# A two-block transformer kernel on one core: the opening's weight splits, relative-bias passes, modulation slots and constant loads put in another order

## The reference, cut to what matters

```python
cond = jax.nn.silu(c)
mod = cond @ w_mod[l] + b_mod[l]            # 1024 x 9216, the chunks of 1024 are sh1, sc1, g1, ...
h = modulate(x, norm_g[l, 0], sh1, sc1)     # rms_norm(x, g) * (1 + sc1) + sh1
x = x + 0.5 * g1[:, None, :] * swiglu(h, w_ffn1_gu[l], w_ffn1_down[l])
```

```python
rel = pos.reshape(B, nb, WINDOW)[..., :, None] - band(pos)[..., None, :]
bias = rel_table[t5_bucket(rel)].astype(jnp.float32)      # 32 buckets, 6 heads
```

## Time and profile before

| | |
|---|---|
| median of 3 runs | 1940.16 us (1939.55 to 1940.95) |
| the profiled execution | 1942.64 us, its span 1940.8 us |
| PE busy | 1832.6 us, 94% |
| DVE busy | 1358.5 us, 70% |
| ACT busy | 931.9 us, 48% |
| mean granted clock of PE | 0.983 |
| HBM read | 436.80 MB, 226 GB/s |

### The profile page before, as it was taken

The page is one execution under the profiler, slowest core; times in us unless marked ns, Lnnn a source line. Parts: engine busy times, 40 slices in busy tenths (PEclk is TensorE's granted clock), DMA queues, the critical chain, the costliest instruction groups (busy, mean ns, idle before and its releaser), DMA issues.

```text
span 1940.8 us, 24233 instructions
## 1 busy us (share of the span) xinstructions
PE 1832.6 (94%) x9181; PEld 1476.7 (76%) x9181; DVE 1358.5 (70%) x1858; ACT 931.9 (48%) x1494; POOL 156.9 (8%) x285
## 2 busy tenths in 40 slices
PE   5999997899999999978999999999999999999997
PEld 2778776778877887766788778877787787877886
DVE  6778776587788787666877774568678765477554
ACT  3334356663345334666544453546433644544443
POOL 2111001011101110010111000000111000000000
PEclk9999998899999999988999999999999999999999
DMA  8889722378977897413889664447898554447652
GB/s 300 327 318 343 273 88 77 109 277 287 342 253 265 299 331 262 128 44 109 308 286 335 231 235 140 157 152 255 288 357 296 194 200 144 157 151 262 206 193 78
DMA packets 241156, 439.50 MB, mean 226 GB/s; under 512 B 15168, under 2 KB 155280, under 8 KB 240912
## 3 DMA queue, kind: packets, MB, share of 16 engines
q1 hardware_dynamic: 204880, 310.92, 47.2%
q0 software_dynamic: 34016, 122.74, 16.6%
q10 hardware_dynamic: 2144, 4.28, 0.6%
HBM read 436.80 MB, written 1.09 MB: 226 GB/s over the span
## 4 chain that ended last, share of the span: by engine, by line
PE 72%; DVE 13%; DMA 7%; ACT 5%; issue 2%; DVEq 0%; SPq 0%; ACTq 0%
PE bank L1623 22%; PE bank L1625 21%; PE bank L1624 21%; DVE weights_lo L1031 6%; DMA arena<-in_w_mod 2%; DMA arena<-in_w_ada 2%; DMA weights_raw<-in_w_ffn_in 2%; PE bank L1798 1%; DVE arena L1143 1%; ACT weights_hi L583 1%; DVE mod_acc L1054 1%; DVE x L1188 1%; DVE arena L1182 1%; PE bank L1737 1%; DVE hT_lo L1152 1%
## 5 line engine op out<-in xcount | busy, mean ns | idle before, releaser
L1031 DVE TENSOR_TENSOR weights_lo<-weights_raw,weights_hi 128x1024 fp32r<-128x1024 f32 (+2 forms) x584 | 672.7, 1201 | 172.3 <-ACT weights_hi L583 171.9
L1623 PE MATMUL bank<-weights_hi,hT_hi 128*128 128x512 f32 x1760 | 696.8, 396 | 19.8 <-DVE hT_lo L1152 6.7
L1625 PE MATMUL bank<-weights_hi,hT_lo 128*128 128x512 f32 x1760 | 684.6, 389 | 0.0
L1624 PE MATMUL bank<-weights_lo,hT_hi 128*128 128x512 f32 x1760 | 682.7, 388 | 0.0
L583 ACT ACTIVATE weights_hi<-weights_raw 128x1024 fp32r<-128x1024 f32 (+2 forms) x584 | 572.1, 1038 | 136.3 <-PE bank L1625 83.3
L1623 PEld LDWEIGHTS bank<-weights_hi,hT_hi 128*128 128x128 f32 x1760 | 330.9, 188 | 104.2 <-issue 13.9
L1625 PEld LDWEIGHTS bank<-weights_hi,hT_lo 128*128 128x128 f32 x1760 | 330.6, 188 | 69.6
L1624 PEld LDWEIGHTS bank<-weights_lo,hT_hi 128*128 128x128 f32 x1760 | 331.2, 188 | 63.7
L757 ACT ACTIVATE actT_hi<-bank 128x512 fp32r<-128x512 f32 x66 | 39.5, 599 | 493.9 <-PE bank L1798 493.9
L1054 DVE SCALAR_TENSOR_TENSOR mod_acc<-arena,silu_cond,mod_acc 128x1024 f32<-128x1024 f32 x184 | 236.2, 1284 | 48.8 <-DMA arena<-in_w_mod 18.0
L1623 PE MATMUL bank<-weights_hi,actT_hi 128*128 128x512 f32 (+1 forms) x544 | 215.6, 396 | 7.2 <-DVE weights_lo L1031 7.2
(11 more groups left out here) (274 smaller groups left out, 1274.2 us busy)
## 6 DMA issues: line engine op xcount, KB each, us to landing
weights_raw<-in_w_ffn_gu SPq DMA_DIRECT2D x176, 512.0 KB, 5.5
arena<-in_w_mod POOLq DMA_DIRECT2D x128, 512.0 KB, 6.7
weights_raw<-in_w_in SPq DMA_DIRECT2D x112, 512.0 KB, 4.7
arena<-in_w_ada POOLq DMA_DIRECT2D x96, 512.0 KB, 6.3
weights_raw<-in_w_ffn_down SPq DMA_DIRECT2D x88, 512.0 KB, 5.2
weights_raw<-in_w_ffn_in SPq DMA_DIRECT2D x88, 512.0 KB, 5.8
weights_raw<-in_w_ffn_out SPq DMA_DIRECT2D x44, 512.0 KB, 4.9
weights_raw<-in_w_out SPq DMA_DIRECT2D x32, 512.0 KB, 4.4
```

The lines of the kernel that those rows point to most:

```text
L1031: V.tensor_tensor(wlo[:, slot, 0:width], raw[:, slot, 0:width], whi[:, slot, 0:width].bitcast(F32), ALU.subtract).then_inc(S("lo_done"), 1)
L1623: T.matmul(o, sh, wh, start=start, stop=False)
L1624: T.matmul(o, sh, wl, start=False, stop=False)
L1625: return T.matmul(o, sl, wh, start=False, stop=stop)
```

## The change

SP now issues 12 modulation units at once as far as slots allow: there are ten places for them, the 4 old slots and the 6 of the weight ring, which is empty then. It then waits until PE has read the first eight, issues the first strip's weights, then the last four modulation units, then waits for all 16 to be read and issues the constants and gains (ACT issued them before), then the second strip.

ACT takes the high parts of all four units of the first strip together, and DVE their low parts together, before DVE stores the second modulation chunk. All six bias passes are in the opening, after units 2, 4, 6, 8, 10 and 12. In each pass PE now adds the three parts itself: three accumulating matmuls of 6 columns in place of one of 18. ACT copies the sums into the table (`bias_copy`), where DVE reduced them. The wait for the constants moves behind the gate/up products of the second strip. The two passes, the reaches, the takes and the part of the mask in the first mixing stage are gone.

```diff
-BIAS_AFTER = (2, 4, 8, 10)
+BIAS_AFTER = (2, 4, 6, 8, 10, 12)
+MOD_AHEAD = 12
...
+            if m < MOD_FIRST_UNITS:
+                same = [i for i in range(m) if first_home(i) == first_home(m)]
+                if same:
+                    eng.wait_ge(S("mod_read"), same[-1] - same[-1] // 8 + 1)
...
+        def first_home(m):
+
+            return m if m < MOD_RING + RING else (m - RING) % MOD_RING if m < 2 * MOD_RING + RING else m - RING
...
+            for m in range(MOD_AHEAD):
+                mod_load(sp, m)
+            sp.wait_ge(S("mod_read"), 7)
+            sp.wait_ge(S("mod_summed"), 1)
+            gu_strip(RING, phases[0][2]["gu"], 0)
+            for m in range(MOD_AHEAD, MOD_FIRST_UNITS):
+                mod_load(sp, m)
             for kind, n0, a in phases:
                 if kind == "ffn":
-                    gu_strip(n0, a["gu"], 0)
+                    if n0 == RING:
+                        sp.wait_ge(S("mod_summed"), 2)
+                        sp.dma_start(con[:, C_FIRST:], A["con"][:, C_FIRST:]).then_inc(S("const_loaded"), 16)
...
-                hi_static(RING, SLOT)
+                for u in range(PREFETCH):
+                    hi_static(RING + u, SLOT)
                 act.wait_ge(S("scale_ready"), 1)
                 x_hi(0)
                 x_hi(1)
-                hi_static(RING + 1, SLOT)
-                x_scaled(a, TRX_FIRST, 2)
-                x_hi(2)
...
+            def bias_copy(q):
+
+                act.wait_ge(S("bias_summed"), q + 1)
+                for g in range(4):
+                    c = P * (q // 2) + 32 * g + 16 * (q % 2)
+                    ins = nc.scalar.activation(bias[:, :, c:c + 16], bank[4 + g][:, 0:16 * WH].rearrange("p (k h) -> p h k", h=WH), ACT.Copy)
+                ins.then_inc(S("bias_taken"), 1)
...
+            for q in range(2, 6):
+                bias_copy(q)
...
             mod_store(0)
-            bias_take(3)
+            bias_reach(5)
+            for u in range(PREFETCH):
+                lo_static(RING + u, SLOT)
             mod_store(1)
...
                 for k in range(16):
-                    for g in range(4):
-                        r = slice(NBUCKET * g, NBUCKET * (g + 1))
-                        ins = T.matmul(bank[4 + g][:, 3 * WH * k:3 * WH * (k + 1)], reached[q % 2][r, k, :], bparts[r].rearrange("p q h -> p (q h)"),
-                                       start=True, stop=True)
+                    for j in range(3):
+                        for g in range(4):
+                            r = slice(NBUCKET * g, NBUCKET * (g + 1))
+                            ins = T.matmul(bank[4 + g][:, WH * k:WH * (k + 1)], reached[q % 2][r, k, :], bparts[r, j], start=j == 0, stop=j == 2)
                 ins.then_inc(S("bias_summed"), 1)
...
-                    pe.wait_ge(S("const_loaded"), 32)
...
+                        if f == 0 and b == 1:
+                            pe.wait_ge(S("const_loaded"), 32)
...
-                        if m == 0 and u in (0, 1):
-                            bias_pass(u + 4)
-                    if m == 0:
-                        pe.wait_ge(S("bias_taken"), 6)
```

More of the change, by code:

```diff
@@ L388, in mod_load @@
             k, was = m % 8, m - MOD_RING
[L389 to L391 removed]
+            if m < MOD_FIRST_UNITS:
+                same = [i for i in range(m) if first_home(i) == first_home(m)]
+                if same:
+                    eng.wait_ge(S("mod_read"), same[-1] - same[-1] // 8 + 1)
+            elif on_pe(was):
                 eng.wait_ge(S("mod_summed"), was // 8 + 1)
@@ L394, in mod_load, with mod_tile @@
                 need(eng, S("mod_used"), taken(was + 1))
-            eng.dma_start(modw[:, m % MOD_RING, :], A[name][layer][k * P:(k + 1) * P, col:col + D]).then_inc(S(mod_sem(m)), 16)
+            eng.dma_start(mod_tile(m), A[name][layer][k * P:(k + 1) * P, col:col + D]).then_inc(S(mod_sem(m)), 16)
+        def first_home(m):
+            return m if m < MOD_RING + RING else (m - RING) % MOD_RING if m < 2 * MOD_RING + RING else m - RING
+        def mod_tile(m):
+            if m < MOD_FIRST_UNITS and first_home(m) >= MOD_RING:
+                return raw[:, first_home(m) - MOD_RING, :]
+            return modw[:, (first_home(m) if m < MOD_FIRST_UNITS else m) % MOD_RING, :]
         def mod_sem(m):
-            return f"first_mod_loaded{m % MOD_RING}" if m < MOD_FIRST_UNITS else f"mod_loaded{m % MOD_RING}"
+            return f"first_mod_loaded{first_home(m)}" if m < MOD_FIRST_UNITS else f"mod_loaded{m % MOD_RING}"
         def mod_wait(eng, m):
-            loads = m // MOD_RING + 1
-            eng.wait_ge(S(mod_sem(m)), 16 * (loads if m < MOD_FIRST_UNITS else loads - MOD_FIRST_UNITS // MOD_RING))
+            same = [i for i in range(m + 1) if mod_sem(i) == mod_sem(m)]
+            eng.wait_ge(S(mod_sem(m)), 16 * len(same))
         block = ctx.enter_context(nc.Block())
@@ L412, in _ @@
             sp.dma_start(ar(A_BIAS, B_END), A["pairs"]).then_inc(S("pos_loaded"), 16)
-            for m in range(MOD_FIRST_UNITS):
-                mod_load(sp, m)
             def gu_strip(n0, w, col):
@@ L1324, in _ @@
                     widths = [512, 512, D_IN - 1536]
-                    if m == 0:
-                        dve.wait_ge(S("hlo_done"), tr[0])
-                        bias_reach(4)
-                        lo_static(n0 + 4, SLOT)
-                        bias_reach(5)
-                        lo_static(n0 + 5, SLOT)
-                        bias_take(4)
-                        lo_static(n0 + 6, SLOT)
-                        bias_take(5)
-                        lo_static(n0 + 7, SLOT)
                     for s in range(3):
-                        for u in range(0 if s == 0 or (s == 1 and m == 0) else 4):
+                        for u in range(0 if s == 0 else 4):
                             lo_static(n0 + 4 * s + u, 2 * widths[s])
@@ L1684, in mod_unit @@
                 mod_wait(pe, m)
-                parts = modw[:, m % MOD_RING, :].rearrange("p (k r j) -> p r k j", r=4, j=32)
+                parts = mod_tile(m).rearrange("p (k r j) -> p r k j", r=4, j=32)
                 for r in range(4):
```

68 lines of the change are left out of this document (28 added, 40 removed).

## The result

The changed kernel takes 1958.94 us (median of 4 runs, 1957.16 to 1963.44); the kernel before took 1940.56 beside it (4 runs, 1939.55 to 1941.31). The ratio is 1.0099, with a 95% interval of 1.0080 to 1.0117. The forecast was 1950, slower, in a range of 1932 to 1959. The sign and the mechanism hold, but the size does not: the time is 8.9 us above the forecast, at the very edge of the range, and the change came out at +18.4 us where +9.8 was forecast (1950 against the 1940.16 on record).

What follows compares the result with a forecast made beforehand. PE, busy 94% of the span, was taken to bound the kernel, so only its standstills count. Profiled 1942.6 + 18.6 - 6.4 - 2.0 = 1952.8, less 2.5 for the profile, rounded to 1950; range 1932 to 1959.

Steps and rivals of the forecast that it cites:

- Passes: Bias passes on PE: each takes 2.0 us without stalls if cost goes by instruction, 0.66 if by columns.
- The chain of pages: Opening: PE stalls for each 256-instruction page, 3.4 us idle or 4.6 loaded; the sixth pass ends at 52.4 us.
- The tail: Opening, ACT and DVE work queued behind the sixth pass: 11.5 us until the first product, at 63.9.
- First strip and clock: First strip's products: 11.5 us, plus 1.3 for the slow clock after PE's idling, bounds 0 and 1.7.
- Mark: Second strip at full speed, closing the opening: 58.1 us before, 76.7 after, 18.6 us later.
- Constants: Wait ahead of the second strip: issued about 54 with over 20 us of cover, so the 3.0 us wait goes.
- Mixing stage: First mixing stage, without its passes, gives back 6.4 us, as its later twin shows; bounds 5 and 6.4.
- Feed-forward between: First feed-forward: weights and units start earlier relative to PE's need, giving 2 us; bounds 0 and 3.
- PE isn't starved: Rival, chance 0.20: PE's reserve exceeds two pages or the stall was chance; 1935, between 1930 and 1939.
- The tail is short as well: Rival, chance 0.05: splits are done ahead of the last unit; first product at 43, time 1928.
- Pages are cheap when PE is starved throughout: Rival, chance 0.15: queues are empty, so a page costs 3.4 us or less; 1942, down to 1938.
- Dearer matmuls: Rival, chance 0.05: small matmuls cost more each, a pass takes 4.2 us; 1946 to 1950.

Runs made afterwards that it cites:

- e5: Kernel before plus 512 smallest matmuls with unused results on PE in the opening, behind the last modulation unit; 1952.53 us beside 1941.29 for before.
- e6: Kernel before plus the same 512 matmuls with unused results, placed in the first mixing stage; 1953.27 us beside 1941.29 for before.
- e10: Kernel after, unchanged, executed and timed again; 1958.56 us beside 1943.24 for before, ratio 1.0082.
- e9: Kernel after with units 12 to 15 moving 128 of 1024 columns and the first strip's weights a quarter; 1955.54 us, ratio 1.0062.
- e4: Kernel after with ACT's table load and four high parts moved ahead of the copies of the last two passes; 1960.25 us, ratio 1.0091.
- e7: Kernel before with constants issued by SP and waited for ahead of the second strip's modulation work; 1939.50 us, ratio 0.9986.
- e1: Kernel after with PE's passes in their old form and summing and copying back on DVE; 1938.10 us, ratio to before 0.9974.
- e8: Kernel before with constants issued by SP, all six passes in the opening, summed by DVE, and four slots; 1935.16 us, ratio 0.9964.
- e2: Kernel after with old 64-matmul passes, ACT copying only one of the three parts; 1937.07 us, ratio to before 0.9970.
- e3: Kernel before with PE adding the three parts (192 matmuls of 6 columns a pass) and DVE copying the sums; 1961.71 us, ratio 1.0099.

## Why the prediction was right in kind and wrong in size

The miss of 8.9 us has two halves. The working went by the profiled execution: it said 1942.6 + 10.2 = 1952.8, and 1957.16 was measured, 4.4 more. The other 4.5 lie in the step from that execution to the median: I took off 2.5, by which the profile of before stood above the median of three runs, and 0.3 by rounding, and the profile of after stands 1.8 below its own median. **That step failed too.** Over more runs the median of before is 1941.29 to 1943.24 (11 to 17 runs each), so the 1942.64 of its profile was no high one, and next to nothing was to be taken off.

The terms of the sum, one by one:

- *Passes.* Taken at 2.0 us without stalls, measured 1.72. The cost goes by instruction, not by column, as chosen; it was the term that mattered least.
- *The chain of pages.* Right as a mechanism, and the page theory is shown by e5 and e6. Borders were forecast at 20.2, 24.8, 28.2, 31.6, 35.6, 40.2, 44.8, 48.8 and 52.2; they came at 18.9, 24.4, 27.7, 31.2, 35.7, 43.4, 48.3, 51.6 and 55.1. The idle price of 3.4 came within 0.1 us four times in this trace; that it was so exact is luck, for the same four pages took 3.6 to 3.9 in e10, and such pages 3.4 to 4.0 in e9. **The step that failed is the loaded price, 4.6 us a page from the one loaded page in the trace of before**: the page asked for at 35.67, just as eight transfers had been or were being issued, took 7.7: its packet started 5.2 us behind the border, where the prediction had 2.2. The sixth pass ended at 55.4 instead of 52.4, +3.0. In e9, with that load cut, the pass ends 3.2 us earlier than in the kernel after, and 4.0 earlier than in e10. The stretch in which it happens was named in the prediction (4.2 MB following from 33.2), yet priced as an ordinary load.
- *The tail.* 11.5 forecast, 11.0 measured (55.4 to 66.4), in the forecast order; e4 shows its cause by removing 5 us of it. It adds -0.5.
- *First strip and clock.* 11.5 + 1.3 forecast, 13.55 measured: +0.75. The granted clock was 0.50 over 65 to 70, and products follow one another in 0.427 us there instead of 0.227; the first twelve products alone lost some 2.5 us, and the bound of 1.7 that I had set was too low. Mark in all: +21.9 for +18.6.
- *Constants.* The wait is gone as forecast; e7 prices it at 0.9 to 2.5 at the boundary, and at a ratio of 0.9986 in time.
- *Mixing stage.* -6.4 forecast, -6.8 measured, and -6.8 again in e1 and e8.
- *Feed-forward between.* -2.0 forecast. From mark to boundary the loss shrank from 21.9 to 20.8, -1.1, and the DMA share over 120 to 160 us fell from 0.95 to 0.86, while PE's busy time there rose only from 37.74 to 38.15. Two executions of before differ by 1.6 at the boundary, so this term can't be told from 2.0.
- *Behind the mixing stage.* Nothing was forecast, and +0.6 came (14.0 at the landmark, 14.6 at the end); e10 has +2.1. It is within what executions of one kernel differ by.

The rivals: *PE isn't starved* fell with the first broken pass. The Trainium skill (Runtime: NRT & Kernel Launch, Instruction fetch mechanics) gives PE room for 2048 instructions. The traces don't agree: with such a reserve e5's 1024 would have run on from the start without a stop, and there are three stops. *The tail is short as well* fell with it. *Pages are cheap when PE is starved throughout* holds in the idle stretches (3.4) and fails where weights are loaded. *Dearer matmuls* fell by the first pass: 192 pairs in 1.72 us, 9 ns a pair. The floor of about 25 ns from start to start in the Trainium skill (TensorE: Matmul & The Clock Gate, Wait — 56ns, not 53.3ns?) would make it 4.8 us, as an estimate; the measured 1.72 decides against it here.

A shorter way to the size, seen only behind the runs: count the pages that are added, and price each at what it moves the boundary (or the length of the mixing stage) by.

| where | pages added | later by (us) | a page |
|---|---|---|---|
| after, opening | 7 | 20.8 | 3.0 |
| after against e2, opening | 6 | 20.2 | 3.4 |
| e3, opening | 4 | 10.4 | 2.6 |
| e5, opening | 4 | 9.9 | 2.5 |
| e3, mixing stage | 2 | 5.6 | 2.8 |
| e6, mixing stage | 4 | 11.8 | 3.0 |

Four passes of 128 instructions against six of 384 are 1792 more, seven pages. The first row also holds what the rest of the change gives or costs in the opening; against e2, which has that rest too, six pages are left, and they cost 3.4 us each. So a page of small instructions costs 2.5 to 3.4 us here. In the mixing stage the two passes cost 6.8 us in their old form, and e3 shows that the new form would have cost 5.6 more there.

## What to carry to other kernels

Count instructions, not only engine time, where a change cuts work into smaller pieces: summing the three parts on PE took from DVE a reduction of 1.55 us a pass, and cost PE a page a pass, six more fetches in the opening at some 3 us each (the seventh comes with the two passes that moved there). A fetch is a small transfer beside all the others, so price it by what was issued just ahead of it, not by a mean load. Before a tail is shortened, look which transfer is next to be late and what else the faster engine sets off: in e4 the second strip's weights, with POOL's loads now issued ahead of them, took back 3.6 of the 5 us. And do not correct a profile by a median of three runs.

## What the runs showed of the hardware

- PE crosses a border every 256 instructions, and where it had less than 3.3 us of work in a page it stopped at each, from the second border of the opening on: in the kernel after, in its second trace, in e4 and e9, and in e5 and e6 on matmuls that compute nothing.
- With the DMA engines idle a page took 3.3 to 3.5 us four times in one trace and 3.4 to 4.0 in others (e9, e10). With transfers newly issued it took 4.5 to 7.7. In the kernel after the difference lies between border and packet (1.1 us idle, 2.2 to 5.2 loaded), not in the fetch itself (2.2 to 2.6 us).
- Four row groups of 32 rows run side by side at 9 ns a matmul with its load (192 in 1.72 us), and neither a smaller column count nor three matmuls adding to the same words changed that much from the 10 ns of 18 columns.
- The granted clock need not be the same in two executions of one program. In the kernel after it was 0.50 over 50 to 55 us, with PE busy 2.41 of 5 us, and again over 65 to 70, behind an idle stretch of 6.29 us. In e10, with the same stops and PE busy 2.35 of 5 us, it stayed at 1.00 until 65 us, and was 0.59 over 65 to 70; what makes the difference no run shows:

```profile
50.00:55.00 5.00, 2.35 (x180) 1.50 (x172) 0.00 (x0) 0.00 (x0) 0.00 (x0) 1.00 0.02 3
65.00:70.00 5.00, 2.83 (x7) 2.28 (x8) 3.00 (x9) 3.66 (x9) 0.00 (x0) 0.59 0.71 242
```
